# Splitting the weight-remainder subtraction of the feed-forward parts between VectorE and GpSimd

## The reference

```python
D_FF = 2816
h = rms_norm(x, ffn_norm_g[l])
u = causal_dwconv(jnp.einsum("bsd,df->bsf", h, ffn_w_in[l]), ffn_conv_w[l]) + ffn_conv_b[l]
gate, up = _split(u, (D_FF, D_FF))
x = x + jnp.einsum("bsf,fd->bsd", jax.nn.silu(gate) * up, ffn_w_out[l])
...
def swiglu(x, w_in, w_out):
    g, u = jnp.split(x @ w_in, 2, axis=-1)
    return (jax.nn.silu(g) * u) @ w_out
```

## Time and profile before

| | us |
|---|---|
| median of 3 runs | 1873.93 (1873.65 to 1875.45) |
| the profiled execution's own time | 1874.18 |
| its span in the profile | 1872.4 |
| PE busy | 1840.0 (98%) |
| DVE busy | 1132.7 (60%) |
| ACT busy | 752.7 (40%) |
| POOL busy | 0.2 |
| granted TensorE clock, mean | 0.997 |

### The profile page before, as it was taken

How to read it: one execution, slowest core, us unless ns; L and a number is a source line. 1 busy time by engine, 2 the same in 40 slices (tenths; PEclk the granted TensorE clock), 3 DMA queues, 4 the chain that set the end, 5 groups by cost and what they waited for, 6 DMA issues and landing times.

```text
span 1872.4 us, 31682 instructions
## 1 busy us (share of the span) xinstructions
PE 1840.0 (98%) x12980; PEld 1702.3 (91%) x12980; DVE 1132.7 (60%) x1777; ACT 752.7 (40%) x961; POOL 0.2 (0%) x4
## 2 busy tenths in 40 slices
PE   9999999999999999999999999999999999999999
PEld 7788999968899999999958887999999999789999
DVE  5556887445588856765427542667557664546763
ACT  3345554223465544333224442433443332334442
POOL 0000000000000000000000000000000000000000
PEclk9999999999999999999999999999999999999999
DMA  6232555423145554455323422455545553244553
GB/s 226 107 118 77 174 188 204 170 90 133 70 138 181 196 200 154 169 185 186 111 112 135 158 83 75 158 172 181 194 147 170 177 190 136 79 153 158 188 210 118
DMA packets 35861, 284.26 MB, mean 152 GB/s; under 512 B 4800, under 2 KB 6976, under 8 KB 8256
## 3 DMA queue, kind: packets, MB, share of 16 engines
q1 hardware_dynamic: 35776, 283.05, 43.0%
HBM read 281.98 MB, written 1.05 MB: 151 GB/s over the span
## 4 chain that ended last, share of the span: by engine, by line
PE 87%; DVE 7%; ACT 4%; issue 1%; DMA 1%; SPq 0%; ACTq 0%; DVEq 0%
PE PS L1236 20%; PE PS L1237 19%; PE PS L1238 19%; PE PS L655 7%; PE PS L763 3%; DVE split L1836 3%; PE PS L1138 2%; PE PS L632 2%; ACT split L1347 2%; PE PS L735 1%; PE PS L1180 1%; PE PS L678 1%; PE PS L698 1%; PE PS L939 1%; PE PS L664 1%
## 5 line engine op out<-in xcount | busy, mean ns | idle before, releaser
L1236 PE MATMUL PS<-Hhi,split 128*128 128x272 f32 (+1 forms) x2144 | 610.9, 285 | 8.7 <-DVE split L1836 7.9
L1836 DVE TENSOR_TENSOR split<-wa,split 128x2048 fp32r<-128x2048 f32 (+1 forms) x174 | 437.0, 2511 | 272.7 <-ACT split L1347 272.6
L1237 PE MATMUL PS<-Hlo,split 128*128 128x256 f32 (+1 forms) x2080 | 591.2, 284 | 0.0
L1238 PE MATMUL PS<-Hhi,split 128*128 128x256 f32 (+1 forms) x2080 | 589.2, 283 | 0.0
L1347 ACT CAST split<-wa 128x2048 fp32r<-128x2048 f32 (+1 forms) x174 | 361.9, 2080 | 145.7 <-PE PS L1238 145.0
L1236 PEld LDWEIGHTS PS<-Hhi,split 128*128 128x128 f32 x2144 | 403.7, 188 | 14.7 <-DVE split L1836 10.7
L1238 PEld LDWEIGHTS PS<-Hhi,split 128*128 128x128 f32 x2080 | 390.9, 188 | 0.0
L1237 PEld LDWEIGHTS PS<-Hlo,split 128*128 128x128 f32 x2080 | 390.6, 188 | 0.2
L1236 PE MATMUL PS<-hidhi,split 128*128 128x256 f32 (+1 forms) x1088 | 310.3, 285 | 6.4 <-DVE hidlo L2453 3.5
L1238 PE MATMUL PS<-hidhi,split 128*128 128x256 f32 (+1 forms) x1088 | 309.0, 284 | 0.0
L1237 PE MATMUL PS<-hidlo,split 128*128 128x256 f32 (+1 forms) x1088 | 308.1, 283 | 0.0
(11 more groups left out here) (312 smaller groups left out, 1958.3 us busy)
## 6 DMA issues: line engine op xcount, KB each, us to landing
wa<-in_wfi SPq DMA_DIRECT2D x126, 1024.0 KB, 4.9
wa<-in_wfo SPq DMA_DIRECT2D x48, 1408.0 KB, 6.1
wa<-in_wmix SPq DMA_DIRECT2D x26, 2048.0 KB, 7.7
wa<-in_wmix SPq DMA_DIRECT2D x4, 1536.0 KB, 6.2
H<-in_wfi SPq DMA_DIRECT2D x3, 1024.0 KB, 9.6
G<-in_wfi SPq DMA_DIRECT2D x3, 1024.0 KB, 4.7
wa<-in_wmix SPq DMA_DIRECT2D x2, 1024.0 KB, 4.7
wa<-in_wmix SPq DMA_DIRECT2D x2, 768.0 KB, 7.9
```

Source lines behind the costliest of these rows:

```text
L1236: pe.matmul(o, hi, xhi, start=first, stop=False)
L1237: pe.matmul(o, hi, xlo, start=False, stop=False)
L1238: return pe.matmul(o, lo, xhi, start=False, stop=last)
L1836: dve.tensor_tensor(out=wlo[n % 2][:, 0:width], in0=wa[:, c % 2, 0:width], in1=whi[n % 2][:, 0:width].bitcast(F32), op=ALU.subtract).then_ ...
```

## The change

The last quarter of each tile's columns (512 of 2048, 704 of 2816) is subtracted by GpSimd into the same `wlo` buffer, and VectorE's instruction covers the first three quarters (1536, 2112). Both wait for the same `w_hi`. GpSimd raises a semaphore of its own, `w_part`; PE, and SP's loads into a slot, wait for both. GpSimd's program is two loops per feed-forward part. For the two tiles that are split early in parts 0, 1 and 5 GpSimd only raises `w_part` with a memset of one column.

```diff
+        def share(width):
+            return width // 4
...
                     name, value = chunks[c - 2][2]
                     sp.wait_ge(FREES[name], value)
+                    if name == "w_lo":
+                        sp.wait_ge(S.w_part, value)
...
                         sp.wait_ge(S.w_lo, 4 * i + (NSPLIT * f + early + r + 1))
+                        sp.wait_ge(S.w_part, 4 * i + (NSPLIT * f + early + r + 1))
...
                     pe.wait_ge(S.w_lo, i + (n + r + 1))
+                    pe.wait_ge(S.w_part, i + (n + r + 1))
...
                         pe.wait_ge(S.w_lo, 4 * i + (n + KF + r + 1))
+                        pe.wait_ge(S.w_part, 4 * i + (n + KF + r + 1))
...
+        @block.gpsimd
+        def _(pool):
+            def part(src, n, width, i=0):
+                at = width - share(width)
+                pool.wait_ge(S.w_hi, i + (n + 1))
+                pool.tensor_tensor(out=wlo[n % 2][:, at:width], in0=src[:, at:width], in1=whi[n % 2][:, at:width].bitcast(F32),
+                                   op=ALU.subtract).then_inc(S.w_part, 1)
+            for f in range(3 * DEPTH):
+                n, early = NSPLIT * f, 2 if f in EARLY else 0
+                c = [source for source, _, _ in chunks].index(("ffn", f, early))
+                for j in range(early):
+                    pool.memset(small[:, 62 + j:63 + j], 0.0).then_inc(S.w_part, 1)
+                n, left = n + early, KF - early
+                with pool.Fori(0, left // 2) as i:
+                    for r in range(2):
+                        part(wa[:, (c + r) % 2, :], n + r, WIN, 2 * i)
+                c, n = c + left, n + left
+                with pool.Fori(0, KD // 2) as i:
+                    for r in range(2):
+                        part(wa[:, (c + r) % 2, :], n + r, WOUT, 2 * i)
...
                 dve.wait_ge(S.w_hi, i + (n + 1))
-                dve.tensor_tensor(out=wlo[n % 2][:, 0:width], in0=wa[:, c % 2, 0:width],
-                                  in1=whi[n % 2][:, 0:width].bitcast(F32), op=ALU.subtract).then_inc(S.w_lo, 1)
+                own = width - share(width)
+                dve.tensor_tensor(out=wlo[n % 2][:, 0:own], in0=wa[:, c % 2, 0:own],
+                                  in1=whi[n % 2][:, 0:own].bitcast(F32), op=ALU.subtract).then_inc(S.w_lo, 1)
```

More of the change, by code:

```diff
@@ L70 @@
 SIGNALS = '''
-    con_in con2_in par_in x_in meta_in pos_in mask_in swa_in wm_in0 wm_in1 out_written wa0 wa1 w_hi w_lo
+    con_in con2_in par_in x_in meta_in pos_in mask_in swa_in wm_in0 wm_in1 out_written wa0 wa1 w_hi w_lo w_part
     dve_chain act_chain rope_ang rope_ready
```

## The result

The change makes the kernel slower: 1890.31 us median (1888.96 to 1893.32) against 1874.13 us of before on the same chip, a ratio of 1.009 (95% interval 1.0077 to 1.0103). That is 0.9% slower, 16.2 us, and clear of the noise. The forecast was 1890.

The account below looks back on a forecast made before the run. PE, busy 98% of the span, was taken to bound the kernel. Terms 7.9 + 4.4 + 2.0 + 1.4 + 0 = 15.7 us, with 1872.4 and 1.8 around the span, gave 1889.9, said as 1890; range 1882 to 1903.

Parts of the forecast that it names:

- The deciding step: Both subtractions read SBUF one after the other, at 60% or more: remainder 0.73 us later, 0.98 for wide tiles.
- first start: First wait of each of six parts, VectorE idle ahead of the subtraction: 0.73 us later each, 4.4 together.
- second start: Second wait with convolution: GpSimd's piece hides behind busy VectorE, the 0.57 us saved pays the earlier 0.73; 0.
- nine loops: Two-tile loops with convolution, no slack, GpSimd first: 0.44 us longer each, 7.9 for 18 in two parts.
- first wide tile: Second product with convolution: PE waits for its first wider tile 0.98 us longer, 2.0 in two parts.
- second wide tile: Second product with convolution: its load goes out later, after the last narrow subtraction; 0.7 us each, 1.4 together.
- The handover: Between rounding and GpSimd's piece, or between the two engines' pieces in turn: 0.1 us.
- Plain parts: Loops have 1.6 us slack; first wide tile 1.0 later, a later 0.95 wait given back: net 0, four parts.
- A: Rival: both subtractions run side by side at solo times, VectorE's sets the end; 13.8 us faster, 1860; 22%.
- B: Rival: GpSimd much slower, 2.29 us for 512 columns, and one after the other; 62 us slower, 1936; 8%.
- C: Rival: a shared rate, each subtraction slows the other, remainder 0 to 0.5 us later; some 7 us, 1881; 12%.
- D: Rival: nothing measurable, GpSimd at 2.3 us side by side ends where VectorE ended before; 1874; 6%.

Follow-up runs that it names:

- the write-only run: Changed kernel, but GpSimd writes zeros into its quarter instead of subtracting and reads nothing; VectorE stays at three quarters: 1858.33 us, ratio 0.9922.
- the control: Changed kernel, but ScalarE rounds in two pieces, last quarter first, and GpSimd still waits for both pieces: 1893.29 us, ratio 1.0100.
- the signals-only run: Changed kernel, but GpSimd only zeroes each remainder tile's last two columns and raises w_part; VectorE subtracts the others: 1873.80 us, ratio 1.0001.
- the run in turn by hand: Changed kernel, but VectorE's piece waits for GpSimd's by w_part, so the two never overlap: 1912.83 us, ratio 1.0212.

## Why the prediction was right

The deciding step, that the pieces run one after the other, was right, and shown: by the stretched rows, by the write-only run against the change (32 us apart with the same split) and by the control. The sum of 15.7 us for a measured 16.2 is partly luck in its terms; part 0 shows how (its late starts are at 184.47, 191.76 and 302.16 before and at 185.38, 193.06 and 308.60 after, and the part began 0.25 later):

| term, per part with convolution | forecast | part 0 |
|---|---|---|
| first start | 0.73 | 0.66 |
| second start | 0 | 0.39 |
| nine loops | 3.95 | 4.55 |
| first wide tile | 0.98 | 0.59 |
| second wide tile | 0.7 | 0.15 |
| sum | 6.4 | 6.3 |

- *GpSimd's duration*, 1.2 for 512 columns, was 1.30 (1.72 for 704).
- *The handover* of 0.1 was two things: 0.08 before GpSimd and -0.14 at VectorE, which ends 1.62 after GpSimd and not 1.76. The two errors cancel: from the end of the rounding to PE's start it is 3.06 (231.78 to 234.84) where it was 2.63 (229.39 to 232.02), 0.43 more for a forecast of 0.44.
- *The loops* grew by more than that, 0.51 each (4.55 in nine). The pair of tiles from which I read 11.46 was one of the short ones, they run from 11.43 to 11.64 and lie at 11.50 on the mean; and 243.48, which I called another such late start, stands only 0.22 after the matmul ahead of it, where 232.02 stands 0.40. After the change a pair takes 11.98 to 12.06 (from 204.87 on), and both its tiles start 0.30 or more after the matmul ahead, not every second one as I wrote. That this is the missing 0.08 is likely, not shown.
- *The second start* I had paid from VectorE's saving, with GpSimd's piece hidden behind a busy VectorE. VectorE was ready there when GpSimd was, and took its turn a second time:

```profile
190.09 1.30 POOL L1801 TENSOR_TENSOR split<-wa,split 128x512 fp32r<-128x512 f32 x1 [4.82 <-ACT split L1356]
...
190.17 2.84 DVE L1871 TENSOR_TENSOR split<-wa,split 128x1536 fp32r<-128x1536 f32 x1
```

- *The second wide tile* was too dear: its later load was hidden by the first wide tile's own delay.
- *Plain parts*: the loops stayed at 6.0 us a tile, and the first wide tile came 0.98 later in part 2 for a forecast of 0.98:

```profile
864.18 0.36 PE L1243 MATMUL PS<-hidhi,split 128*128 128x272 f32 x1 [0.98 <-POOL split L1801]
```

  PE's wait behind the two wide subtractions has gone, as forecast, because VectorE went first. Parts 3 and 4 together cost 1.1 and part 5 0.6, forecast 1.5 and 0.7.
- *Terms put at nothing*: the second semaphore costs nothing (the signals-only run), and GpSimd's first subtraction, at 182.41, took 2.86 beside VectorE's 1.76, where later ones took 2.84 to 2.93, so no first-time cost shows. For the loads my own numbers leave 0.3 us and not about 1 (11.4 less 5.5 less 4.9 less 0.7); one narrow load was waited for by ScalarE, 1.64 us before 1737.88, and PE did not feel it.
- *Not in the sum*: the mixers moved by -1.8 and +2.6 us with their code unchanged, 0.7 together; they go with TensorE's clock, below.

Of the rivals, A's price (13.8 us faster) was close to what the write-only run gave, 15.4, though its condition did not hold. B's slow GpSimd, C's rate and D's 2.3 us side by side did not occur.

## What to carry to other kernels

VectorE and GpSimd are not two independent engines for tensors in SBUF: when VectorE's instruction has two SBUF inputs and GpSimd's has one or two, they run in turn, as all the float32 pairs that met here did, and moving columns from the faster to the slower makes the sum longer. Relief by GpSimd pays where its piece can lie under VectorE's PSUM reads, its idle time, or waits for a third engine; splitting the producer's work so that GpSimd's part is ready first made 16 us slower into 15 us faster. In these profiles such a collision is a row that is longer than its solo time and not idle time, so compare an instruction's shortest and longest rows before reading the waits.

## What the runs showed of the hardware that was not expected

After PE had stood idle for 1.90 us before 542.81 in the changed kernel, its matmuls went on at 0.12 us and then, from 543.67, at 0.21 us, till 546.87; the granted clock of that stretch:

```profile
core 0: us, PE busy (x) PEld busy (x) DVE busy (x) ACT busy (x) POOL busy (x), PEclk, DMA share, GB/s
540.00:545.00 5.00, 3.10 (x21) 2.93 (x21) 4.48 (x6) 1.43 (x4) 2.71 (x1) 0.85 0.22 36
545.00:550.00 5.00, 5.00 (x37) 5.00 (x36) 4.89 (x8) 2.86 (x4) 1.30 (x1) 0.81 0.43 179
```

It is the lower of the clock's two levels (1.2 GHz) for some 3 us. The kernel before idled 1.24 us at the same place and stayed at 1.00. The drop cost nothing there, since the next wait took it up (the next tile's first matmul starts 0.54 after the one ahead of it at 550.49; at the same place of part 0 it is 2.10), but in the mixer before part 5 the changed kernel has two such stretches and the kernel before none, which goes with the +2.6 us. And where it has one stretch of 3.4 us less than the kernel before, in the mixer before part 3, it is 1.8 us faster. The new waits are not needed for such a stretch: the signals-only run, whose feed-forward parts take as long as those of before, has one in the mixer before part 5 too (103.2 us there, and 258.2 before part 3). Nor is a wait of that length enough: in the changed kernel the waits of 1.90, 1.83 and 1.84 us before 185.38, 193.06 and 308.60 were followed by none. In the run in turn by hand eight of the nine stretches begin within 1.3 us after PE took up again from a wait of 1.76 us or more. What decides is left open.

GpSimd's float32 subtraction alone took 0.74 us for 256 columns, 1.30 for 512, 1.72 for 704, 1.87 for 768 and 2.38 for 1024; its memset of 512 took 0.53, its copy 0.62.
